# Attention outputs normalised by pairs of tiles, pooled channels ahead of them and first in the projection, first gate's rows through memory

## What is computed

```python
mod = silu(cond) @ w_ada + b_ada          # shift_a, scale_a, gate_a, shift_f, scale_f, gate_f
h = rmsnorm(x) * (1 + scale_a) + shift_a
q, k, v, g, za_f, za_b, u = split(h @ w_in)
o = gla_fwd(q, k, v) + gla_bwd(q, k, v)   # chunked, 4 heads of 128 channels
o = o * rsqrt(mean(o * o)) * gla_norm_g * silu(g)
p = pooled(u) @ w_pool * pool_scale       # 4 groups of 128 channels
y = concat([o, p]) @ w_out
x = x + gate_a * y
x = x + gate_f * moe(rmsnorm(x) ...)      # 16 experts, 80 slots each, then a final norm
```

## Time and profile before

| | us |
|---|---|
| median of 3 runs | 1903.52 (1901.79 to 1906.2) |
| the profiled execution | 1903.08 |
| its span, first to last instruction | 1901.3 |
| PE busy in the span | 1847.0 (97%) |
| DVE busy | 1551.7 (82%) |
| ACT busy | 1250.7 (66%) |
| first expert matmul | 393.06 |

### The profile page before, as it was taken

One profiled execution on the slowest core, in us unless ns is written; L12 is line 12 of the kernel. 1 busy time (PEld: TensorE's weight loads), 2 busy tenths in 40 slices (PEclk: granted clock), 3 DMA queues, 4 the chain that ended last, 5 costly groups with the idle time before them and its releaser, 6 DMA issues.

```text
span 1901.3 us, 25073 instructions
## 1 busy us (share of the span) xinstructions
PE 1847.0 (97%) x9056; PEld 1500.9 (79%) x9056; DVE 1551.7 (82%) x1254; ACT 1250.7 (66%) x1002; POOL 272.7 (14%) x120
## 2 busy tenths in 40 slices
PE   6998879999999999999999999999999999999998
PEld 2777667668888888888888888888888888888886
DVE  4632854689889898989898989898989898989897
ACT  4433642356767676767676767676767677777774
POOL 1000000010202030303030302030303030303060
PEclk9999989989999999999999999999999999999999
DMA  8522532689999999999999999999999999999993
GB/s 287 178 76 85 184 128 89 221 313 390 389 384 390 384 381 385 368 385 373 386 372 387 372 386 371 383 373 387 375 382 374 385 372 387 372 383 370 393 378 123
DMA packets 280812, 622.83 MB, mean 328 GB/s; under 512 B 12461, under 2 KB 46018, under 8 KB 280778
## 3 DMA queue, kind: packets, MB, share of 16 engines
q1 hardware_dynamic: 273664, 598.68, 85.8%
q0 software_dynamic: 6064, 20.72, 3.7%
q10 hardware_dynamic: 1050, 2.97, 0.4%
HBM read 607.19 MB, written 15.14 MB: 327 GB/s over the span
## 4 chain that ended last, share of the span: by engine, by line
PE 93%; DVE 4%; ACT 1%; issue 1%; DMA 0%; ACTq 0%; DVEq 0%
PE bank L1831 17%; PE bank L1832 17%; PE bank L1835 17%; PE bank L1861 8%; PE bank L1857 8%; PE bank L1856 8%; PE bank L1416 3%; PE bank L1418 3%; PE bank L1417 3%; PE bank L1841 1%; PE bank L1451 1%; PE bank L1661 1%; DVE w_lo L945 1%; PE bank L1468 0%; PE bank L1469 0%
## 5 line engine op out<-in xcount | busy, mean ns | idle before, releaser
L1278 DVE TENSOR_TENSOR w_lo<-raw,w_hi 128x2048 fp32r<-128x2048 f32 x528 | 1197.7, 2288 | 121.7 <-ACT w_hi L845 119.6
L845 ACT CAST w_hi<-raw 128x2048 fp32r<-128x2048 f32 x524 | 997.8, 1913 | 181.2 <-PE bank L1835 104.3
L1831 PE MATMUL bank<-w_hi,xe_hi 128*128 128x512 f32 (+1 forms) x1536 | 573.8, 380 | 0.0
L1832 PE MATMUL bank<-w_hi,xe_lo 128*128 128x512 f32 (+1 forms) x1536 | 563.4, 373 | 0.0
L1835 PE MATMUL bank<-w_lo,xe_hi 128*128 128x512 f32 (+1 forms) x1536 | 380.4, 373 | 0.0
L1831 PEld LDWEIGHTS bank<-w_hi,xe_hi 128*128 128x128 f32 x1536 | 290.0, 189 | 49.6 <-issue 1.7
L1832 PEld LDWEIGHTS bank<-w_hi,xe_lo 128*128 128x128 f32 x1536 | 290.3, 189 | 48.5
L1835 PEld LDWEIGHTS bank<-w_lo,xe_hi 128*128 128x128 f32 x1536 | 273.4, 188 | 51.8
L1857 PE MATMUL bank<-w_hi,hT_lo 128*128 128x512 f32 x700 | 273.0, 390 | 0.0
L1856 PE MATMUL bank<-w_hi,hT_hi 128*128 128x512 f32 x700 | 272.7, 390 | 0.0
L597 POOL DMA_INDIRECT acc_dram<-yrow,idx_s x15 | 43.6, 2910 | 1072.6 <-DVE yrow L1320 1072.6
(11 more groups left out here) (264 smaller groups left out, 1367.6 us busy)
## 6 DMA issues: line engine op xcount, KB each, us to landing
raw<-in_w_e_gate SPq DMA_DIRECT2D x176, 1024.0 KB, 11.0
raw<-in_w_e_up SPq DMA_DIRECT2D x176, 1024.0 KB, 11.3
raw<-in_w_e_down SPq DMA_DIRECT2D x176, 1024.0 KB, 10.9
raw<-in_w_ada SPq DMA_DIRECT2D x16, 1024.0 KB, 5.1
raw<-in_w_in SPq DMA_DIRECT2D x8, 1024.0 KB, 5.6
ada_f<-in_w_ada SPq DMA_DIRECT2D x4, 1024.0 KB, 16.6
raw<-in_w_out SPq DMA_DIRECT2D x4, 1024.0 KB, 5.0
ada_raw<-in_w_ada SPq DMA_DIRECT2D x4, 1024.0 KB, 12.2
```

The source lines that it names most:

```text
L845: nc.scalar.copy(hi_slot(j), raw[:, raw_slot(j), :]).then_inc(hi_done, 1)
L1278: nc.vector.tensor_tensor(lo_slot(j), raw[:, raw_slot(j), :], hi_slot(j), ALU.subtract).then_inc(lo_done, 1)
L1831: nc.tensor.matmul(out, xe_hi[:, kk, :], wh[:, k, :], start=kk == 0, stop=False)
L1832: nc.tensor.matmul(out, xe_lo[:, kk, :], wh[:, k, :], start=False, stop=False)
```

## The change

What was one step for all five tiles becomes steps for tiles 0 and 1, 2 and 3, and 4: squares and root on ACT, reciprocal and norm on DVE. The four pooled products go ahead of the attention rows, into banks 5, 2, 7, 1 with the context in 4, and are evacuated there. ada(9) moves between the rows of tiles 1 and 2; the rows of tile 2 wait for the eight pooled `m_lo`. In `mix` the column blocks are rotated by four (`mix_at`), so that the pooled channels overlay q k and u. The projection of tile 0, first half, starts with the pooled channels (kh = 1) ahead of the heads' transposes, which go to banks 5, 3, 4, 7 and 2. The broadcasts on PE and the copies on ACT are gone: POOL writes the 2 x 1024 values of gate_a to memory and reads each row back into all partitions. The brow product stands behind PE's wait for `m_hi` and `m_lo`.

```diff
-        ojunk = at("ojunk", [P, P], F32, DR)
+        ojunk = at("ojunk", [P, P], F32, EX + K_POOL * 4 + 2 * KB)
+        def mix_at(m):
+
+            return (m + HEADS) % KD
...
+        POOL_MIX, POOL_CTX = ((4, 5), (6, 2), (7, 7), (5, 1)), 4
+        HEAD_MIX, HEAD_CTX = ((0, 5), (1, 3), (2, 4), (3, 7)), 2
...
+            pool.wait_ge(mod_done, ADA_FIRST + 3)
+            for st in range(2):
+                pool.dma_start(gate_dram[st].rearrange("(k p) -> p k", p=P), modT[:, 16:24, st], allow_slow_non_contiguous=True).then_inc(gate_out, 16)
+            pool.wait_ge(gate_out, 32)
+            pool.wait_ge(g_s1, TILES)
+            for st in range(2):
+                pool.dma_start(gate_a[:, st, :], gate_dram[st:st + 1, :].broadcast_to([P, D])).then_inc(gate_in, 16)
...
+            def mix_high(blocks, ctx_bank, done):
+
+                for q, (m, b) in enumerate(blocks):
+                    act.wait_ge(m_ps, done + q + 1)
+                    nc.scalar.activation(mix[:, 0:T_LAT, 0, mix_at(m), :], bank[b][:, :].rearrange("p (t n) -> p t n", t=T_LAT),
+                                         ACT.Copy, scale=mix_scale(m)).then_inc(m_hi, 1)
+                act.wait_ge(m_ps, done + HEADS + 1)
+                for m, _ in blocks:
+                    h = m % HEADS
+                    nc.scalar.activation(mix[:, T_LAT, 0, mix_at(m), :], bank[ctx_bank][:, h * P:(h + 1) * P], ACT.Copy, scale=mix_scale(m)).then_inc(m_hi, 1)
+
+            def o_squares(tiles):
+
+                act.wait_ge(o_ps, tiles[-1] + 1)
+                for t in tiles:
+                    for h in range(HEADS):
+                        nc.scalar.activation(ojunk[:, :], o_bank(t, h % 2)[:, h // 2, :], ACT.Square,
+                                             accum_out=ss[:, t * HEADS + h:t * HEADS + h + 1]).then_inc(o_sq, 1)
+                        act.wait_ge(o_sq, t * HEADS + h + 1)
+                cols = slice(tiles[0] * HEADS, tiles[-1] * HEADS + HEADS)
+                nc.scalar.activation(rstd[:, cols], ss[:, cols], ACT.Sqrt, bias=eps[:, :], scale=1.0 / DV).then_inc(o_rt, 1)
+
+            mix_high(POOL_MIX, POOL_CTX, 0)
+            o_squares((0, 1))
             high(WOUT0 + 1)
+            high(WOUT0 + 2)
             mod_rows(9)
-            high(WOUT0 + 2)
...
+            o_squares((2, 3))
+            o_squares((4,))
+            mix_high(HEAD_MIX, HEAD_CTX, HEADS + 1)
             high(WOUT0 + 3)
...
+            def o_norm(tiles, pair):
+
+                dve.wait_ge(o_rt, pair + 1)
+                cols = slice(tiles[0] * HEADS, tiles[-1] * HEADS + HEADS)
+                step(nc.vector.reciprocal(rstd[:, cols], rstd[:, cols]))
+                for t in tiles:
+                    dve.wait_ge(evac_act, 9 + t + 1)
+                    for par in range(2):
...
+            mix_low(POOL_MIX, POOL_CTX, 0)
+            o_norm((0, 1), 0)
             low(WOUT0 + 1)
             low(WOUT0 + 2)
+            o_norm((2, 3), 1)
+            o_norm((4,), 2)
             mod_columns(9)
...
+            mix_low(HEAD_MIX, HEAD_CTX, 2 * HEADS)
...
-            dve.wait_ge(gate_sb, 4)
+            dve.wait_ge(gate_in, 32)
             dve.wait_ge(x_back, 32)
...
+            for m, b in POOL_MIX:
+                nc.tensor.matmul(bank[b][:, :], wpool[:, m - HEADS, :], pT[:, m - HEADS, 0:L_LAT], start=True, stop=True).then_inc(m_ps, 1)
...
+            pe.wait_ge(scan_done, HP)
+            o_rows(0)
+            o_rows(1)
+            ada(9)
+            pe.wait_ge(m_lo, 2 * HEADS)
+            o_rows(2)
+            o_rows(3)
+            o_rows(4)
             ada_turn(9)
...
-            for q in range(4):
-                if q == 1:
-                    pe.wait_ge(mod_done, 11)
-                if q >= 2:
-                    pe.wait_ge(gate_sb, q - 1)
-                for j in range(4):
-                    last = same_rows(bank[5 + q % 2][:, j * P:(j + 1) * P], 16 + 4 * (q % 2) + j, q // 2, P)
-                last.then_inc(gate_ps, 1)
-
-            pe.wait_ge(gate_sb, 4)
...
+                turned_over = t == 0 and half == 0
+                start = kh == int(turned_over)
+                if t >= 2 and start and ks[0] == 0:
                     pe.wait_ge(wo_ev, 2 * (t - 2) + half + 1)
...
+                    last = product(bank[2 * (t % 2) + half][:, :], mix[:, t, 0, mix_at(kk), :], mix[:, t, 1, mix_at(kk), :], wh[:, k, :], wl[:, k, :],
+                                   start and k == 0, not start and k == 3)
...
+            pe.wait_ge(o_n, 2)
+            pe.wait_ge(m_hi, 2 * HEADS)
+            mixed(0, 0, 1, every)
+
+            pe.wait_ge(o_n, T_LAT)
+            for m, b in HEAD_MIX:
+                if b == 7:
+                    pe.wait_ge(o_n, TILES)
+                for t in range(T_LAT):
+                    last = nc.tensor.transpose(bank[b][:, t * P:(t + 1) * P], on[:, t, m, :], ident)
+                last.then_inc(m_ps, 1)
...
             for t in range(T_LAT):
                 mixed(t, 0, 0, every)
-                mixed(t, 0, 1, every)
+                if t >= 1:
+                    mixed(t, 0, 1, every)
```

More of the change, by code:

```diff
@@ L1647, in _, with o_rows @@
             pe.wait_ge(p_sb, TILES)
-            ada(9)
-            pe.wait_ge(scan_done, HP)
             pe.wait_ge(mod_done, ADA_FIRST + TILES + 1)
-            for t in range(TILES):
+            for m, b in POOL_MIX:
+                nc.tensor.matmul(bank[b][:, :], wpool[:, m - HEADS, :], pT[:, m - HEADS, 0:L_LAT], start=True, stop=True).then_inc(m_ps, 1)
+            for m, _ in POOL_MIX:
+                h = m - HEADS
+                last = nc.tensor.matmul(bank[POOL_CTX][:, h * P:(h + 1) * P], wpool[:, h, :], pT[:, h, L_LAT:NTOK], start=True, stop=True)
+            last.then_inc(m_ps, 1)
+            def o_rows(t):
                 for h in range(HEADS):
@@ L1713, in mixed @@
                     kk = 4 * kh + k
-                    last = product(bank[2 * (t % 2) + half][:, :], mix[:, t, 0, kk, :], mix[:, t, 1, kk, :], wh[:, k, :], wl[:, k, :], kk == 0, kk == KD - 1)
+                    last = product(bank[2 * (t % 2) + half][:, :], mix[:, t, 0, mix_at(kk), :], mix[:, t, 1, mix_at(kk), :], wh[:, k, :], wl[:, k, :],
+                                   start and k == 0, not start and k == 3)
                 if ks[-1] == 3:
@@ L1717, in mixed @@
                         last.then_inc(unit_used, 1)
-                    elif kh == 1:
+                    elif not start:
                         last.then_inc(wo_ps, 1)
```

97 lines of the change are left out of this document (28 added, 69 removed).

## The result

The changed kernel takes **1892.99 us** (median of 5 runs, 1891.68 to 1893.83) where the kernel before took 1903.52 beside it: a ratio of 0.9943, 95% interval 0.9931 to 0.9956, so 10.5 us or 0.57% faster. The forecast was 1891.8 us with a range of 1889.0 to 1897.0 and 0.92 on faster. The profiled execution took 1892.61 us; its span is 1889.7 us.

A forecast was written before the change was run, and what follows sets the result against it. PE was taken to bound the kernel, with 93% of the span. The projection goes on at 286.3 with 2.8 us done, as if begun at 283.5 instead of 295.26: 1903.5 − 11.7 = 1891.8 us, range 1889 to 1897.

The forecast's parts named there:

- The order and its times: PE, ACT and DVE from pooling to projection, timed step by step: projection as if begun at 283.5, 11.7 us earlier.
- the clock falls: Rival: PE drops to half speed after the new idle gap before the projection, costing 2 us; 1893.8 us, chance 0.28.
- The small writes: POOL's 4-byte gate writes during the scan: cost taken as nothing, at most 7.7 us; rival shared with late x2, chance 0.14.
- The slack of 4.5 us: In the scan, the w_ada load issued at 215.91 lands at 221.0, and ACT casts it only at 225.56.
- Gates off PE and ACT: First listed cause of the 11.7 us: gate broadcasts and copies removed, and with them the wait on `gate_sb`.
- x2 late: Rival: x2's reload, with 2.5 us of cover left, delays the first residual; shared with the small writes, chance 0.14.
- The writes hold the engines for long (the slower case): Rival: small writes hold DMA engines 24.4 us, delaying a w_ada load in the scan; 1911.7 us, slower, chance 0.04.
- The table load: ACT's table load of 1.28 us leaves the path; the skill's 2.66 us would make the removed part 1.2 us larger.
- More is hidden than counted: Rival: tile 4's squares and norm run nearer to PE, DVE's evacuations end up to 1.5 us sooner; 1890.3, chance 0.08.

The follow-up runs named there:

- gates_late: Changed kernel with POOL's whole gate block (small writes and broadcasts) moved behind the output of the scan's last states; 1891.74 us.
- gates_twice: Changed kernel with the two writes of 4-byte pieces issued a second time after the first two landed; 1900.02 us.
- after_again: The changed kernel, unaltered, measured once more as a control; 1894.22 us.
- after_third: The changed kernel, unaltered, measured a third time for comparison; 1892.81 us.
- gates_only_late: Kernel before with only the gate rows sent through memory by POOL, that block behind the state outputs; 1902.51 us, ratio 0.9992 to the kernel before.
- quarter_back: Changed kernel with the pooled quarter of tile 0's projection put back behind the heads' one; 1898.8 us.
- gates_only: Kernel before with only the gate rows sent through memory by POOL, writes at the early place; 1908.28 us, ratio 1.0027 to the kernel before.
- after: The changed kernel itself, first measurement, against the kernel before; 1892.99 us, ratio 0.9943.
- no_pairs: Changed kernel with one root, one reciprocal and one norm step for all five tiles again; 1902.93 us, ratio 1.0001 to the kernel before.

## Why the prediction was right, point by point

- **The order and its times.** Held to within half a microsecond, step by step: pooled products at 248.49; turn of the modulation row to 277.0; quarter to 279.85 (279.8 forecast); first pair's table load at 264.20; second root at 275.94; `mod_columns(9)` done and DVE at its first evacuation of the projection's input at 281.56 (282.0); DVE's end at 285.3 (285.8); projection at 285.90 (286.3). With the quarter done, 2.7 us at full clock, the projection stands 295.26 − (285.90 − 2.7) = 12.1 us earlier; 11.7 were forecast.
- **The clock.** This step failed. The forecast kept 2.4 GHz over the gap, and the rival "the clock falls" (0.28) is what came, in all three traces of the kernel, in gates_late and in gates_twice. The gap was 2.89 us and not 3.2. Its price of 2 us was mis-sized by little: 1.6. What the prediction had read as evidence against it (35 dense us ahead of the gap) was no protection.
- **The small writes.** Taken at 0, with bounds of 0 and 7.7. With the broadcasts behind them they cost 0.8 to 1.4 us. That is the term of the sum that was mis-sized. The slack of 4.5 us was read rightly: the load landed 13.4 us after its issue and not 5.3, 8.1 later; less the slack that is 3.6, and ACT's cast waited 3.61 us for it. What the working lacked is that PE doesn't pay such a wait whole. PE waited 0.98 us for ACT's row and started the pooling 13.32 us behind O where it was 11.79, so 1.53 later, and then did it in 6.89 us and not in 7.66, since less of it fell on the lower clock (granted 0.60 in 243 to 246, before 0.50): 0.76 us are left. The argument for 0, that `wrt`'s 6.1 us was mostly not its own, doesn't carry over to pieces of 4 bytes.
- **Sum of these for the profiled executions**: 12.1 up to the projection, − 1.6 for the clock, − 0.8 for the writes (here), + 0.8 because the scan's last turn started earlier in this execution, + 1.05 from X to E: 11.55, and the spans differ by 11.6. Outside the span stand 2.9 us of the profiled execution after and 1.8 before, so its time is 10.5 earlier. In other executions of the changed kernel the 1.05 (after_again) or the 0.8 (after_third) are missing; the 1.05 are the clock of four matmuls ahead of the experts, and no effect of the change. The median came within 1.2 us of the forecast, and of the two errors that make 2.4 to 3.0 us, 0.4 were given back by a projection that starts sooner than forecast and about 1 by what varies from run to run. So the range held, but that the number came so near is luck: the rival with the falling clock (1893.8) lies nearer to the 1893.0 than the forecast does, and names what happened.
- **By cause.** "Gates off PE and ACT" stood first in the list of causes and is worth nothing alone (gates_only_late, ratio 0.9992 with 1 in its interval). Whether it is worth something in the changed kernel, where PE no longer waits at that place, was not tried. The pairs are worth 9.0 us of P to X and the quarter 5.0, if one of them is taken away from the whole. That is more than the 10.5 between the kernels, since whichever is taken away opens a gap, and the clock falls behind it. The pooled products' move was not tried by itself.
- **x2 late**: it was not. The reload is issued at 277.04 and 277.79, and the first residual at 290.64 waited for PE's bank alone.
- **The writes hold the engines for long (the slower case)**: 16.2 us would have used up the gain; a second pair of writes cost 6.0 us on PE's path, a quarter of the rival's 24.4. The rule of the Trainium skill ("DMA: Bandwidth & Descriptors", Specifications), that pieces under 512 bytes are read, modified and written, is in line with engines that are half busy at 32 to 43 GB/s, but no run here shows that this is why.
- **The table load**: in the row the root follows 1.30 us after the start of the load, and the load follows the squares at once. The further drain of the Trainium skill ("ScalarE: Activation LUTs", What ACT_TABLE_LOAD costs; 2.66 us for a switch) is not to be seen.
- **More is hidden than counted**: true for 0.4 us (projection at 285.90), not for 1.5.

## What to carry to other kernels

Work that stands in a wait of its engine is not worth removing by itself; move what the wait waits for, and count the gap that stays behind for what it does to the clock of the work after it. When work is put into one gap, look for the next place where that work had been cover (here 12 matmuls ahead of a transpose). The small writes with their broadcasts cost nothing 40 us later, where the DMA engines were idle, so place such transfers by the load on the queues and not by when their data are ready.

## What the runs showed of the hardware

- **Writes of 4 bytes**: two of 1024 pieces, 8 KB together, landed 9.3 us after issue, and 1 MB loads issued behind them landed after 13.4 and 13.9 us instead of 5.3 and 5.2. Writing them twice made the distance from O to P 6.0 us longer. With no load beside them they landed after 8.7 us, of which the DMA engines were half busy for 2 us and then idle (gates_late).
- **PE's clock behind a gap** of 2.44 to 3.01 us fell in quarter_back (2.44), gates_only (2.54), after (2.89), after_again, after_third, gates_late and gates_twice (2.90 each) and no_pairs (3.01), and held over 2.53 us in the kernel before and in gates_only_late. Length alone doesn't decide between 2.44 and 2.54. What stood ahead differs, but not in one way: in quarter_back PE went into the gap at 1.2 GHz, in gates_only it had come back to 2.4 GHz some 2 us later than in the two that held, and in after it had been at 2.4 GHz and busy for 35 us. No run here finds the rule. The Trainium skill ("TensorE: Matmul & The Clock Gate", Part 1) says of the slow matmuls at a kernel's start that their number varies between runs of one kernel; the traces agree in kind, with 2.02 us in one trace of the changed kernel and 3.78 in another (after_again) for the same four matmuls.
- **Small shifts** of a microsecond early in the program come out as 1 us more or less at the experts' start, from the clock of the few matmuls there (2.02 to 3.78 us for the same four). It limits what one run can tell; distances between marks repeat to 0.1 us where no clock changes in them.
